# A gated mixer on one core: the u and gate columns in groups of 1024, one of four turns as seven block products

## The chip, the cores and the metric

One Trainium2 chip, one of its cores. The metric is the device time of one execution in microseconds (us), lower is better. TensorE (PE) multiplies, ScalarE (ACT) and VectorE (DVE) work element by element, GpSimd (POOL) does four small reciprocal roots, SyncE (SP) issues most of the DMAs.

## The reference, cut to what matters

Two blocks run one after the other over 256 tokens of width 2048, all in float32. The change lies in the first block:

```python
h = rmsnorm(x, a_norm)                       # (256, 2048)
z = h @ w_in                                 # w_in: (2048, 12288)
u, v, gate = jnp.split(z, 3, axis=-1)        # 4096 columns each
u = gelu(u); v = rmsnorm(gelu(v), v_gain)
sv = einsum('gpq,bnqgc->bnpgc', w_s, vc) + b_s     # 8 groups of 512 columns, chunks of 128 tokens
y = u * sv
x = x + (y * silu(gate)) @ w_out             # w_out: (4096, 2048)
```

Then follow the final norm of that block and a second block (attention, an mLSTM, a gated feed-forward net), which the change touches only in the signs of some sums.

## The kernel before

**Float32 products from three passes.** Every weight and every activation is split in a high part, rounded to TensorE's reduced float32 type (ACT, a copy), and a low part, the rest (DVE, a subtraction). A product is hi x hi + hi x lo + lo x hi: three matmuls.

**Items.** The weights come as chunks of 256 rows x 512 columns, laid out as 128 x 1024 elements (512 KB). PE goes through them as one list, ITEMS, stage by stage: v, ug, out1, vv, side, gm0 ..., down. An item of a plain chunk is 12 matmuls of 512 columns: 2 row tiles x 2 token tiles x 3 passes. A ring has RING = 4 places for w_hi and w_lo: ACT makes the high part of item n + 4 (`high_of_chunk`) once PE has ended item n (`mm_done`), DVE then makes its low part (`low_of_chunk`, L1432), and PE starts item n + 4 when `lo_ready` says so. Each engine's program is one list: what an engine does besides stands at a fixed place, behind its step for an item (`split(stage, k)` is the step that prepares item k + 4).

**Seven products for eight.** In some turns of the stages v, out1, gm0, gm1, out2 and down, four chunks (a 512 x 1024 block of weights, split as B11, B12, B21, B22) are multiplied by the Strassen-Winograd scheme: seven block products of 6 matmuls each in place of four chunks of 12. For this DVE makes four sums of weight blocks in place (`block_sum`, L1437), and the result needs sums of products: 1, 5, 6 and 7 have PSUM banks of their own (XS), and `own_products` adds them up.

**The stage ug** has none of this. Eight groups i of 512 columns: 8 chunks of u columns (PSUM banks G[0]), then 8 chunks of gate columns (G[1]). The PE side is `one("ug", ...)` with `tokens` (L556). Beside it run, per group: the high and low part of v (`v_hi`, `v_lo`) and of the scaled `w_s` (`scale_ws`, `ws_hi`, `ws_lo`); `spatial(i)`, six matmuls into SV (XS banks 2 and 3, L713); t1 = SV * gain (L1627); gelu of u straight from PSUM (ACT, L1029); t1 = (t1 + b_s) * u (L1632); tanh of the gate straight from PSUM; t2 = (t2 + 1) * gate (L1636); t1 = t1 * scale * t2, two halves (L1640), which is y; then y is turned by eight transposes (`y_turned`, L604, into TR, XS banks 0 and 1) and split in `y_high` and `y_low`.

**What is queued.** SP issues the load of a chunk into the ring place that `lo_ready` frees. Nothing else orders the engines but semaphores.

Of the kernel before, what the change touches and what calls it, by code (L numbers as in the profile page):

```python
# [5 lines left out]
P = 128  # L6
S = 256
D = 2048
# [94 lines left out]

PLAIN = ("C0", "C1", "C2", "C3")
# [5 lines left out]
for _name, _counts in PHASES:  # L110
    FIRST_ITEM[_name] = len(ITEMS)
    if _name not in WIDE_STEPS:
        ITEMS += [Item(_name, None, 0, None, None, _k) for _k in range(sum(_counts))]
        continue
# [11 lines left out]
CHUNK_ITEMS = [n for n, item in enumerate(ITEMS) if not item.product]  # L126
# [12 lines left out]

RESULT_OF = {2: 0, 4: 1, 3: 2}  # L140

GAIN_AT = {FIRST_ITEM["ug"] + (-24, -8, 14, 30, 46, 62, 78, 94)[i]: i for i in range(GROUPS)}
BLOCKS_AT = {FIRST_ITEM["v"] + 8: ("v", B11), FIRST_ITEM["v"] + 9: ("v", B12),
# [41 lines left out]

def buffer_of(q, b):

    return b if b == B21 else (b + q - quads_ahead(QUADS[q][0])) % 3


def sum_slot(phase, turn):

    return SUM_TURNS["gm0" if phase == "gm1" else phase].index(turn)
# [36 lines left out]
def group_of(phase, g):  # L230


    n = FIRST_GROUP[phase] + g
    if phase in WIDE_STEPS:
# [28 lines left out]
def build(nc, x, x_tokens, stream, w_s, params, gain_rows, final_rows, gate_w, identity, consts, out):  # L263
# [25 lines left out]
    class Wide:  # L289
# [3 lines left out]
        def __init__(self, sb, name, blocks, hi, lo, rows, sums, u):  # L293
# [8 lines left out]

    norm_in = Norm("in", "a_norm")
# [6 lines left out]
    x_junk = sb("x_junk", "y", 48 * kib, [P, 2, D])  # L310
    v_wide = Wide(sb, "v", [("y", 0), ("y", 4 * kib), ("y", 8 * kib), ("y", 12 * kib)],
                  [("y", 16 * kib), ("y", 20 * kib)], [("y", 24 * kib), ("y", 28 * kib)], ("y", 92 * kib), ("mix", 4 * kib),
                  ("y", 32 * kib))
    v_junk = sb("v_junk", "y", 48 * kib, [P, 2, COLS])

    u_act = sb("u_act", "x", 0, [P, 2, COLS])
# [5 lines left out]
    v_all = sb("v_all", "y", 64 * kib, [P, 2, E])  # L322

    v_hi = sb("v_hi", "y", 28 * kib, [P, 2, COLS], F32R)
    v_lo = sb("v_lo", "y", 60 * kib, [P, 2, COLS], F32R)
# [75 lines left out]
    wide = {"v": v_wide, "out1": out1_wide, "gm0": gm_wide, "gm1": gm_wide, "out2": out2_wide, "down": down_wide}  # L401
    u_sum = sb("u_sum", "mix", 4 * kib, [P, 4, S])

# [5 lines left out]
    ws_scaled = sb("ws_scaled", "small", off + 2 * kib, [P, 2, P])  # L409
# [62 lines left out]
    with block:  # L472

        @block.sync
        def _(sp):
# [10 lines left out]
            def load_block(q, b):  # L486

                phase, g, turn = QUADS[q]
                half = 1 if b in (B12, B22) else 0
                row = 2 * turn + (1 if b in (B22, B21) else 0)  # L490
                sp.dma_start(wide[phase].blocks[buffer_of(q, b)][:], stream[chunk_in_stream(phase, g, half, row)]).then_inc(
                    block_full[b], 16)


            for n, item in enumerate(ITEMS):
                if item.product in NEXT_IN_PLACE and quad_of(item) + 1 < len(QUADS):
                    q = quad_of(item)
                    if QUADS[q + 1][0] == item.phase:
                        sp.wait_ge(lo_ready, n + 1)
                        load_block(q + 1, NEXT_IN_PLACE[item.product])  # L500
                if not item.product and CHUNK_COUNT[n] + RING < len(CHUNK_ITEMS):
# [4 lines left out]
                if n in BLOCKS_AT:  # L506
# [15 lines left out]
                    if phase == "out1" and b == B21:  # L522

                        sp.wait_ge(sem["y_turned"], GROUPS)
# [16 lines left out]
        def _(pe):  # L541
# [87 lines left out]
            def opens_own(item):  # L629
# [3 lines left out]
                if new:  # L633
                    opened.add(key)
                    if own_ahead(item.phase, item.group):
# [23 lines left out]
            def wide_product(item, a_hi, a_lo, slot):  # L659

                p, i = item.product, sum_slot(item.phase, item.turn)
                sums = wide[item.phase]
                own = {1: 0, 5: 1, 6: 2, 7: 3}
# [34 lines left out]
            def y_turned(i):  # L698
# [5 lines left out]
                blocks_turned(t1).then_inc(sem["y_turned"], 1)  # L704

            def spatial(i):
                pe.wait_ge(sem["v_lo_ready"], i + 1)
                pe.wait_ge(sem["ws_lo_ready"], i + 1)
                if i:
                    pe.wait_ge(sem["sv_read"], i)  # L710
                for t in range(2):
                    for n, (w, a) in enumerate(((ws_hi, v_hi), (ws_hi, v_lo), (ws_lo, v_hi))):
# [3 lines left out]
            for i in range(GROUPS):  # L716
                for k in range(8):
                    one("ug", 2 * i, k, tokens("ug", 2 * i, norm_in.hi, norm_in.lo))
                    if i and k == 4:
                        y_turned(i - 1)  # L720
                if i == 0:

                    pe.wait_ge(sem["own_read"], own_ahead("ug"))
                spatial(i)
                for k in range(8):
                    one("ug", 2 * i + 1, k, tokens("ug", 2 * i + 1, norm_in.hi, norm_in.lo))
# [266 lines left out]
        def _(act):  # L993
# [3 lines left out]
            def high_of_chunk(n):  # L997

                item = ITEMS[n]
                if item.product:  # L1000
                    b, uses = PRODUCT_OF[item.product], quad_of(item)
                    of = wide[item.phase].blocks[buffer_of(uses, b)]
                    if item.product in (1, 3, 2):
                        act.wait_ge(block_full[b], 16 * (uses + 1))
                    else:
                        act.wait_ge(sem["block_sums"], 4 * uses + {5: 1, 7: 2, 6: 3, 4: 4}[item.product])
# [62 lines left out]
            def sums_high(phase, n):  # L1069

                if n - 2 in SUMS_AT[phase]:
                    i = SUMS_AT[phase].index(n - 2)
                    act.wait_ge(sem["sums_ready"], sums_ahead(phase) + i + 1)
                    activation(wide[phase].sums_hi[i][:], wide[phase].sums[:], ACT.Copy).then_inc(sem["sums_hi_ready"], 1)

            def first_product(phase, n):

                for name, g in GROUPS_BY_PRODUCTS:
# [3 lines left out]
                    if n == product_item(phase, g, turn, 6):  # L1082
                        act.wait_ge(mm_done, product_item(phase, g, turn, 1) + 1)
                        if phase == "out1" and g == 0:

                            act.wait_ge(sem["v_lo_ready"], GROUPS)
# [25 lines left out]
                        activation(wide[phase].p1[:], XS[:, 0, :], ACT.Copy).then_inc(sem["p1_ready"], 1)  # L1112

            def v_taken(q):

                product, read, _ = done("v", q)
                activation(v_all[:, :, col_block(q)], product, ACT.Copy).then_inc(read, 1)

            def v_gelu(q):

                act.wait_ge(group_read[q % 2], q // 2 + 1)
                at_v = v_all[:, :, col_block(q)]
                by_token(at_v, at_v, ACT.Gelu_apprx_tanh, scale).then_inc(sem["v_ready"], 1)

            def v_squares(q):
# [4 lines left out]
                for t in range(2):  # L1130
                    ins = activation(v_junk[:, t, :], v_all[:, t, col_block(q)], ACT.Square, accum_out=v_ss[:, t, q:q + 1])
# [39 lines left out]
            for i in range(GROUPS):  # L1171
                for k in range(16):
                    split("ug", 16 * i + k)
                    if i == 0 and k < 2:
                        v_gelu(6 + k)
                        v_squares(6 + k)
                    if k == 1:

                        if i:
                            act.wait_ge(sem["sv_ready"], i)  # L1180
                        activation(v_hi[:], v_all[:, :, col_block(i)], ACT.Copy).then_inc(sem["v_hi_ready"], 1)
                    if k == 4:
                        act.wait_ge(sem["ws_scaled"], i + 1)
                        activation(ws_hi[:], ws_scaled[:], ACT.Copy).then_inc(sem["ws_hi_ready"], 1)
                    if i and k == 4:
                        y_high(i - 1)
                    if k == 7:
                        product, read, _ = done("ug", 2 * i)
                        if i:
                            act.wait_ge(sem["u_used"], i)  # L1190
                        by_token(u_act, product, ACT.Gelu_apprx_tanh, scale).then_inc(read, 1)
                product, read, _ = done("ug", 2 * i + 1)
                if i:
                    act.wait_ge(sem["y_ready"], i)
                by_token(t2, product, ACT.Tanh, scale_half).then_inc(sem["gate_t_ready"], 1)
# [936 lines left out]
```

## Time and profile before

| | |
|---|---|
| median of 3 runs | 2097.87 us (2097.86 to 2098.11) |
| span of the profiled execution, first to last instruction | 2095.9 us |
| PE busy, LDWEIGHTS busy | 2089.8 us (100%), 1750.1 us (84%) |
| DVE busy, ACT busy | 1506.6 us (72%), 1112.4 us (53%) |
| DMA | 404.40 MB, mean 193 GB/s |

The profiled execution's time is given as its span alone. The median of the timed runs is 1.97 us above it, which is taken as what lies ahead of the first and behind the last instruction. An engine's busy time counts its instructions; matmuls overlap, so that their durations (390 ns) are longer than the distance from one to the next. In a timeline each row is a start, a duration, the engine, the line, the operation, and in brackets the idle time before it with what ended it.

### The profile page before, as it was taken

How to read it: one execution, taken by the hardware profiler on the slowest of the kernel's cores; microseconds unless marked ns; L12 is line 12 of the kernel's file. 1: busy time of each engine (PE TensorE's matmuls, PEld its weight loads, DVE VectorE, ACT ScalarE, POOL GpSimd, SP SyncE). 2: the span in 40 equal slices, each digit the busy share in tenths (PEclk: the TensorE clock that was granted, in tenths of full speed). 3: DMA queues.
4: the chain of work that ended last, by engine and by line, in shares of the span. 5: the costliest groups of instructions: out<-in, count | busy, mean ns of one | idle time of the engine just before them, and what ended most of it. 6: DMA issues, size and time to landing. Idle time of an engine off the chain costs nothing.

```text
span 2095.9 us, 25218 instructions
## 1 busy us (share of the span) xinstructions
PE 2089.8 (100%) x10000; PEld 1750.1 (84%) x10000; DVE 1506.6 (72%) x1702; ACT 1112.4 (53%) x1314; POOL 17.5 (1%) x17
## 2 busy tenths in 40 slices
PE   9999999999999999999999999999999999999999
PEld 7888888888888887888888888888888888888887
DVE  7987656655787754665669678867777777779986
ACT  6765444444456544555455454555555555555553
POOL 0000000000000000100000000000000000000000
PEclk9999999999999999999999999999999999999999
DMA  8665555555764555544465656556556566556663
GB/s 337 210 200 175 198 187 187 194 187 189 272 214 157 194 194 171 177 155 153 150 210 181 221 169 208 167 185 192 187 185 195 183 192 190 181 181 232 224 203 133
DMA packets 111957, 404.40 MB, mean 193 GB/s; under 512 B 12512, under 2 KB 13280, under 8 KB 111328
## 3 DMA queue, kind: packets, MB, share of 16 engines
q1 hardware_dynamic: 109440, 394.66, 57.1%
q10 hardware_dynamic: 2400, 8.14, 1.0%
q8 instruction: 79, 1.29, 0.3%
q14 instruction: 38, 0.31, 0.0%
HBM read 400.65 MB, written 2.10 MB: 192 GB/s over the span
## 4 chain that ended last, share of the span: by engine, by line
PE 96%; DVE 3%; ACT 1%; DMA 0%; issue 0%; ACTq 0%; DVEq 0%
PE g L556 37%; PE g L653 23%; PE xs L581 8%; PE g L581 8%; PE xs L676 5%; PE xs L585 4%; PE g L585 4%; PE g L680 4%; DVE w_lo L1432 1%; PE xs L604 1%; PE xs L713 1%; ACT w_hi L1014 0%; PE xs L833 0%; DMA xf<-in_x 0%; PE xs L830 0%
## 5 line engine op out<-in xcount | busy, mean ns | idle before, releaser
L1432 DVE TENSOR_TENSOR w_lo<-raw,w_hi 128x1024 fp32r<-128x1024 f32 x659 | 803.4, 1223 | 492.6 <-ACT w_hi L1014 486.9
L1014 ACT ACTIVATE w_hi<-raw 128x1024 fp32r<-128x1024 f32 x659 | 697.4, 1059 | 756.6 <-PE g L556 411.7
L556 PE MATMUL g<-w_hi,mid_both 128*128 128x512 f32 x1024 | 326.7, 394 | 0.0
L556 PE MATMUL g<-w_hi,in_both 128*128 128x512 f32 x1024 | 318.8, 390 | 0.1
L556 PEld LDWEIGHTS g<-w_hi,in_both 128*128 128x128 f32 x1024 | 192.2, 188 | 40.3 <-DVE v_all L1564 0.5
L556 PEld LDWEIGHTS g<-w_hi,mid_both 128*128 128x128 f32 x1024 | 192.3, 188 | 39.6
L556 PE MATMUL g<-w_lo,mid_both 128*128 128x512 f32 x512 | 199.4, 389 | 0.0
L556 PE MATMUL g<-w_lo,in_both 128*128 128x512 f32 x512 | 199.2, 389 | 0.0
L581 PE MATMUL g<-mlp_both,w_hi 128*128 128x512 f32 x704 | 176.8, 393 | 0.0
L581 PE MATMUL xs<-mlp_both,w_hi 128*128 128x512 f32 x704 | 176.3, 392 | 0.0
L581 PEld LDWEIGHTS g<-mlp_both,w_hi 128*128 128x128 f32 x704 | 126.5, 189 | 22.8
L581 PEld LDWEIGHTS xs<-mlp_both,w_hi 128*128 128x128 f32 x704 | 126.6, 189 | 22.6
L653 PE MATMUL g<-w_hi,in_both 128*128 128x512 f32 x352 | 112.6, 390 | 1.3 <-DVE w_lo L1500 1.0
L556 PEld LDWEIGHTS g<-w_lo,in_both 128*128 128x128 f32 x512 | 96.1, 188 | 19.7
L556 PEld LDWEIGHTS g<-w_lo,mid_both 128*128 128x128 f32 x512 | 96.3, 188 | 19.1
L585 PEld LDWEIGHTS g<-mlp_both,w_lo 128*128 128x128 f32 x704 | 96.2, 190 | 7.0
L585 PEld LDWEIGHTS xs<-mlp_both,w_lo 128*128 128x128 f32 x704 | 96.0, 190 | 6.9
L585 PE MATMUL g<-mlp_both,w_lo 128*128 128x256 f32 x704 | 98.3, 282 | 0.0
L585 PE MATMUL xs<-mlp_both,w_lo 128*128 128x256 f32 x704 | 98.2, 282 | 0.0
L653 PE MATMUL g<-w_hi,f_hi 128*128 128x512 f32 x240 | 93.7, 390 | 0.2
L653 PE MATMUL g<-w_hi,f_lo 128*128 128x512 f32 x240 | 93.4, 389 | 0.0
L653 PE MATMUL g<-w_lo,f_hi 128*128 128x512 f32 x240 | 93.4, 389 | 0.0
(404 smaller groups left out, 3044.3 us busy)
## 6 DMA issues: line engine op xcount, KB each, us to landing
raw<-in_stream SPq DMA_DIRECT2D x659, 512.0 KB, 3.5
d_block<-in_stream SPq DMA_DIRECT2D x28, 512.0 KB, 4.6
o_block<-in_stream SPq DMA_DIRECT2D x24, 512.0 KB, 4.7
v_block<-in_stream SPq DMA_DIRECT2D x20, 512.0 KB, 4.4
gm_block<-in_stream SPq DMA_DIRECT2D x12, 512.0 KB, 5.1
x_first<-in_x_tokens ACTq DMA_DIRECT2D x2, 1024.0 KB, 6.8
gain_row<-in_gain_rows SPq DMA_DIRECT2D x8, 256.0 KB, 3.5
xt<-in_x_tokens ACTq DMA_DIRECT2D x1, 2048.0 KB, 8.0
```

The costliest lines, as they stand in the source:

```text
L556: ins = mm(G[buf][:, t, :], a[:, kt, at_t], w[:, slot, j * COLS:(j + 1) * COLS], start=(kt == 0 and n == 0), stop=(last and j == ROWS_PER_ ...
L581: mm(UP[buf][:, b, :, :], w_hi[:, slot, j * COLS + b * P:j * COLS + (b + 1) * P], a_both[:, :, kt, :], start=(kt == 0), stop=False, skip_g ...
L585: ins = mm(UP[buf][:, b, 0, :], w_lo[:, slot, j * COLS + b * P:j * COLS + (b + 1) * P], a_both[:, 0, kt, :], start=False, stop=(last and j ...
L604: ins = turn(TR[:, b, t * P:(t + 1) * P], of[:, t, b * P:(b + 1) * P], ident[:])
L653: ins = mm(GG[:, bank, :], a[:, kt, t * P:(t + 1) * P], w[:, slot, half_chunk(j)], start=n == 0 and opens(item, bank), stop=ended and n == ...
L676: ins = mm(XS[:, own[p], :], a, w[:, slot, half_chunk(j)], start=first and opens_own(item), stop=last and j == 1 and n == 2, skip_group_ch ...
L680: ins = mm(GG[:, RESULT_OF[p], :], a, w[:, slot, half_chunk(j)], start=first and opens(item, RESULT_OF[p]), stop=False, skip_group_check=True)
L713: ins = mm(SV[:, t, :], w[:, t, :], a[:, t, :], start=(n == 0), stop=(n == 2))
L1014: activation(w_hi[:, n % RING, :], of[:], ACT.Copy).then_inc(hi_ready, 1)
L1432: v.tensor_tensor(w_lo[:, n % RING, :], of, w_hi[:, n % RING, :].bitcast(F32), ALU.subtract).then_inc(lo_ready, 1)
```

## The change

- Stage ug: per group of 512 u and 512 gate columns (1024 together) the sixteen chunks are four turns of four (C0 and C1 are u columns, C2 and C3 gate columns); turn 2 is done as seven products. 19 items in a fixed order in place of 16.
- DVE makes the four block sums of each group; products 1, 5, 6 and 7 go to banks of XS that SV and TR also use; `ug_own_products` adds them up into `act` and `gate` (SBUF), `u_result` and `gate_result` add what stands in G[0] and G[1]. gelu and tanh read those SBUF tiles, not PSUM.
- The work beside moves: `spatial(i)` from the middle of the group to behind its first item, `y_turned` behind its fourth, the last two steps of y (`gate_times`, `y_product`) from the end of a group to behind the first split of the next; `ws_scaled` falls away (ACT scales while it rounds).
- In every stage the block sums are additions where they were subtractions, with the signs of the products' sums to match; some buffers lie elsewhere.

```diff
+UG_TURN = 2
+UG_FIRST = ((0, "C0"), (0, "C1"), 1, (0, "C2"), 5, (0, "C3"), (1, "C0"), (1, "C1"), 7, 6, (1, "C2"), (1, "C3"),
+            3, 2, 4, (3, "C0"), (3, "C1"), (3, "C2"), (3, "C3"))
+UG_ORDER = ((0, "C0"), (0, "C1"), (0, "C2"), (0, "C3"), 1, (1, "C0"), 5, (1, "C1"), (1, "C2"), (1, "C3"), 7, 6,
+            (3, "C0"), (3, "C1"), 3, 2, 4, (3, "C2"), (3, "C3"))
+UG_HALF_ENDS = (16, 18)
+UG_OWN_BANK = {1: 2, 5: 3, 6: 0, 7: 1}
...
+                    if item.phase == "ug" and item.group and item.product in (1, 5):
+                        pe.wait_ge(sem["sv_read"], item.group + 1)
+                    elif item.phase == "ug" and item.group:
+                        pe.wait_ge(sem["y_lo_ready"], item.group)
...
+            for n in range(items_of("ug")):                      # PE
+                i, k = divmod(n, UG_ITEMS)
...
+                step(item, norm_in.hi, norm_in.lo, at_item % RING).then_inc(mm_done, 1)
+                if k == (0 if i else 14):
+                    spatial(i)
+                if i and k == 3:
+                    y_turned(i - 1)
...
+            for n in range(items_of("ug")):                      # ACT
+                i, k = divmod(n, UG_ITEMS)
+                split("ug", n)
...
+                first_product("ug", FIRST_ITEM["ug"] + n)
+                if k == UG_HALF_ENDS[0]:
+                    u_gelu(i)
+                if k == UG_HALF_ENDS[1]:
+                    gate_t(i)
...
-                v.tensor_tensor(to[:], a[:], b[:], ALU.subtract).then_inc(sem["block_sums"], 1)
+                v.tensor_tensor(to[:], a[:], b[:], ALU.add).then_inc(sem["block_sums"], 1)
...
+            def ug_own_products(i, k):                           # at_6 is item 11 (9 in group 0)
+                if after == 0:
+                    link(v.tensor_tensor(g.u_a, g.p1, p6, ALU.subtract))
+                if after == 1:
+                    link(v.tensor_tensor(g.u_b, p7, g.u_a, ALU.add))
+                if after == 2:
+                    link(v.tensor_tensor(g.u_a, p5, g.u_a, ALU.add))
+                if after == 3:
+                    v.tensor_tensor(g.u_d, p5, g.u_b, ALU.add).then_inc(sem["own_read"], 1)
...
+            for n in range(items_of("ug")):                      # DVE
+                i, k = divmod(n, UG_ITEMS)
+                if k == UG_HALF_ENDS[0]:
+                    u_result(i)
+                if k == UG_HALF_ENDS[1]:
+                    gate_result(i)
+                split("ug", n)
...
+                if i and k == 0:
+                    gate_times(i - 1)
+                    y_product(i - 1)
+                if k == (1 if i else 15):
+                    sv_gained(i)
+                if i and k == 4:
+                    y_low(i - 1)
+                if k == (6 if i else 16) and i + 1 < GROUPS:
+                    low(v_lo[:, i + 1], v_all[:, i + 1], v_hi[:], "v_hi_ready", i + 2, "v_lo_ready")
+                if k == (7 if i else 17) and i + 1 < GROUPS:
+                    ws_low(i + 1)
+                ug_own_products(i, k)
+                if k == 17:
+                    u_times(i)
```

`block_sums`, which `split` calls, is unchanged in its places: the first sum stands behind the low part of product 1, the second behind that of the item after it, the third behind product 5, the fourth behind product 6. `link` is an instruction followed by a wait for its own end. The last comments of some lines are put in here for the reader.

## Rows read from the trace of the kernel before

**Rows 1.** The page: busy times, TensorE's granted clock, the chain that ended last.

```profile
PE 2089.8 (100%) x10000; PEld 1750.1 (84%) x10000; DVE 1506.6 (72%) x1702; ACT 1112.4 (53%) x1314; POOL 17.5 (1%) x17
...
PEclk9999999999999999999999999999999999999999
...
PE 96%; DVE 3%; ACT 1%; DMA 0%; issue 0%; ACTq 0%; DVEq 0%
```

**Rows 2.** Busy time by engine in one ug group: length, PE, PEld, DVE, ACT.

```profile
224.22:269.99 45.77, 45.77 (x208) 37.99 (x206) 27.48 (x27) 21.45 (x23) 0.00 (x0) 1.00 0.57 190
```

**Rows 3.** Timeline of PE in the same group: transposes, six matmuls of spatial.

```profile
235.10 1.03 PE L604 MATMUL xs<-ident,t 128*128 128x128 f32 x8
...
244.15 0.39 PE L713 MATMUL xs<-v_hi,ws_hi 128*128 128x512 f32 x1
...
245.51 0.39 PE L556 MATMUL g<-w_hi,in_both 128*128 128x512 f32 x1
```

**Rows 4.** Groups of DVE instructions, whole span: busy us, mean ns, idle before.

```profile
L1437 DVE TENSOR_TENSOR v_block<-v_block,v_block 128x1024 f32<-128x1024 f32 x20 | 24.5, 1224 | 1.4
...
L1632 DVE SCALAR_TENSOR_TENSOR t<-t,par,u_act 128x1024 f32<-128x1024 f32 x8 | 10.2, 1278 | 0.0
...
L1564 DVE TENSOR_TENSOR v_all<-g,v_u 128x512 f32<-128x512 f32 x12 | 7.7, 683 | 0.7 <-DVE v_u L1554 0.5
```

**Rows 5.** Timeline of DVE in ug.

```profile
245.50 1.23 DVE L1432 TENSOR_TENSOR w_lo<-raw,w_hi 128x1024 fp32r<-128x1024 f32 x1 [1.50 <-ACT w_hi L1014]
...
269.85 1.22 DVE L1636 SCALAR_TENSOR_TENSOR t<-t,g 128x1024 f32<-128x1024 f32 x1
271.11 1.42 DVE L1640 SCALAR_TENSOR_TENSOR t<-t,scale_half,t 128x512 f32<-128x512 f32 x2
272.44 1.22 DVE L1432 TENSOR_TENSOR w_lo<-raw,w_hi 128x1024 fp32r<-128x1024 f32 x1
```

**Rows 6.** Timeline of DVE in stage v, where seven products are in use.

```profile
57.64 1.22 DVE L1432 TENSOR_TENSOR w_lo<-v_block,w_hi 128x1024 fp32r<-128x1024 f32 x1
58.96 1.23 DVE L1437 TENSOR_TENSOR v_block<-v_block,v_block 128x1024 f32<-128x1024 f32 x1
60.10 1.22 DVE L1432 TENSOR_TENSOR w_lo<-v_block,w_hi 128x1024 fp32r<-128x1024 f32 x1
...
70.39 1.23 DVE L1437 TENSOR_TENSOR v_block<-v_block,v_block 128x1024 f32<-128x1024 f32 x1
...
173.24 0.68 DVE L1546 TENSOR_TENSOR v_u<-xs,v_u 128x512 f32<-128x512 f32 x1
173.96 1.23 DVE L1432 TENSOR_TENSOR w_lo<-raw,w_hi 128x1024 fp32r<-128x1024 f32 x1
175.10 1.28 DVE L1564 TENSOR_TENSOR v_all<-g,v_u 128x512 f32<-128x512 f32 x2
```

**Rows 7.** Timeline of ACT in stages v and ug.

```profile
66.73 1.32 ACT L1029 ACTIVATE v_all<-v_all,scale 128x512 f32<-128x512 f32 x2
67.95 1.04 ACT L1014 ACTIVATE w_hi<-v_block 128x1024 fp32r<-128x1024 f32 x1
...
71.65 1.06 ACT L1014 ACTIVATE w_hi<-v_block 128x1024 fp32r<-128x1024 f32 x1 [0.47 <-DVE v_block L1437]
...
244.41 1.06 ACT L1014 ACTIVATE w_hi<-raw 128x1024 fp32r<-128x1024 f32 x1 [1.66 <-PE g L556]
```

**Rows 8.** Weight loads of PE where stage ug begins.

```profile
176.44 0.19 PEld L556 LDWEIGHTS g<-w_hi,in_both 128*128 128x128 f32 x1 [0.51 <-DVE v_all L1564]
176.55 0.19 PEld L556 LDWEIGHTS g<-w_lo,in_both 128*128 128x128 f32 x1
176.78 0.19 PEld L556 LDWEIGHTS g<-w_hi,in_both 128*128 128x128 f32 x1
```

More of the change, by code:

```diff
@@ L124, with in_ring @@
 ITEM_AT = {item: n for n, item in enumerate(ITEMS)}
-CHUNK_ITEMS = [n for n, item in enumerate(ITEMS) if not item.product]
+def in_ring(item):
+    return not item.product
+CHUNK_ITEMS = [n for n, item in enumerate(ITEMS) if in_ring(item)]
 CHUNK_COUNT = {n: c for c, n in enumerate(CHUNK_ITEMS)}
@@ L233, in group_of @@
     n = FIRST_GROUP[phase] + g
-    if phase in WIDE_STEPS:
+    if phase in WIDE:
         end = half_end(phase, g // 2, g % 2) + 1
@@ L486, in load_block @@
             def load_block(q, b):
[L488 to L492, printed above, removed]
+                phase, g, _ = QUADS[q]
+                sp.dma_start(wide(phase, g).blocks[buffer_of(q, b)][:], stream[block_row(q, b)]).then_inc(block_full[b], 16)
             for n, item in enumerate(ITEMS):
-                if item.product in NEXT_IN_PLACE and quad_of(item) + 1 < len(QUADS):
+                if next_in_place(item) is not None and quad_of(item) + 1 < len(QUADS):
                     q = quad_of(item)
@@ L661, in wide_product @@
                 p, i = item.product, sum_slot(item.phase, item.turn)
-                sums = wide[item.phase]
-                own = {1: 0, 5: 1, 6: 2, 7: 3}
+                sums = wide(item.phase, item.group)
+                own = UG_OWN_BANK if item.phase == "ug" else OWN_BANK
                 last = item.turn == last_by_products(item.phase, item.group)
@@ new lines, in v_high, with ws_high @@
+            def v_high(i):
+                if i:
+                    act.wait_ge(sem["sv_ready"], i)
+                activation(v_hi[:], v_all[:, i], ACT.Copy).then_inc(sem["v_hi_ready"], 1)
+            def ws_high(i):
+                if i:
+                    act.wait_ge(sem["sv_ready"], i)
+                else:
+                    act.wait_ge(sem["v_rstd_ready"], 1)
+                    act.wait_ge(sem["ws_in"], 16)
+                for t in range(2):
+                    ins = activation(ws_hi[:, t, :], ws_t[:, i, :], ACT.Copy, scale=v_stat[:, 4 + t:5 + t])
+                ins.then_inc(sem["ws_hi_ready"], 1)
@@ new lines, in u_gelu, with gate_t @@
+            def u_gelu(i):
+                _, end, read = group_of("ug", 2 * i)
+                act.wait_ge(group_read[0], read)
+                by_token(gated[i].act, gated[i].act, ACT.Gelu_apprx_tanh, scale).then_inc(sem["u_act_ready"], 1)
+            def gate_t(i):
+                _, end, read = group_of("ug", 2 * i + 1)
+                act.wait_ge(group_read[1], read)
+                if i:
+                    act.wait_ge(sem["y_turned"], i)
+                by_token(t2, gated[i].gate, ACT.Tanh, scale_half).then_inc(sem["gate_t_ready"], 1)
@@ L1426, in low_of_chunk @@
                 item = ITEMS[n]
-                if item.product:
-                    of = wide[item.phase].blocks[buffer_of(quad_of(item), PRODUCT_OF[item.product])][:]
+                if not in_ring(item):
+                    of = wide(item.phase, item.group).blocks[buffer_of(quad_of(item), PRODUCT_OF[item.product])][:]
                 else:
@@ new lines, in u_result, with gate_result @@
+            def u_result(i):
+                buf, end, read = group_of("ug", 2 * i)
+                dve.wait_ge(mm_done, end)
+                dve.wait_ge(sem["own_read"], own_ahead("ug", i + 1))
+                v.tensor_tensor(gated[i].act[:], G[0], gated[i].act[:], ALU.add).then_inc(group_read[0], 1)
+            def gate_result(i):
+                buf, end, read = group_of("ug", 2 * i + 1)
+                dve.wait_ge(mm_done, end)
+                v.tensor_tensor(gated[i].gate[:], G[1], gated[i].gate[:], ALU.subtract).then_inc(group_read[1], 1)
@@ L1693, in _ @@
                 if n == 0:
+                    gate_times(GROUPS - 1)
+                    y_product(GROUPS - 1)
                     dve.wait_ge(mm_done, FIRST_ITEM["out1"])
```

298 lines of the change are left out of this document (164 added, 134 removed).

## The prediction

> **What bounds the kernel now.** I read the page's busy table first: PE is busy for 100% of the span at the full granted clock, and the chain that ended last runs through PE for 96% of it [rows 1]. So time comes off only where PE issues fewer matmuls, and goes on only where PE has to wait. Then the stage windows: one ug group lasts 45.77 us, PE is busy in all of it, DVE in 27.48 us, which is 60% [rows 2]. Then the timelines, for the distances from start to start, because busy times overlap. Six matmuls of 512 columns take 245.51 - 244.15 = 1.36 us, 0.2267 each [rows 3]. Sixteen chunks of 12, 43.52 us, and `spatial`, 1.36, leave 0.89 us of the 45.77 for the eight transposes. These three are the whole group.
>
> **What the change takes off.** Four of a group's sixteen chunks (48 matmuls) become seven products of 6 (42). Six matmuls less is 1.36 us, for eight groups 48 matmuls, **10.88 us**. Nothing else of PE's work changes: `spatial` and `y_turned` move and cost the same.
>
> **What it adds on DVE.** Per group, three low parts more (19 for 16), four block sums, four sums of products of 512 columns (0.68 each), `u_result` and `gate_result` (like L1564, two halves of 0.68, here one instruction of 1024; the 1024-element rows take 1.22), less `ws_scaled` and its low part in two forms that about cancel. That is 3 x 1.22 + 4 x 1.22 + 4 x 0.68 + 2 x 1.22 = 13.7 us [rows 4, 5]. DVE goes from 27.5 to 41.2 us in a group of 44.42 (45.77 less 1.36, rounded), 93%. On average that fits. Whether PE waits hangs on the order, as neither DVE nor ACT can be more than four items ahead of PE.
>
> **Distances used.** Low part behind low part or behind a block sum 1.14 (58.96 to 60.10); block sum behind a low part, whose end it waits for, 1.32 (57.64 to 58.96); a 512-column sum with a wait for its end 0.72 (173.24 to 173.96), without one 0.60 (the pair of 1.28 less one of 0.68) [rows 4, 6]. `gate_times` to `y_product` 1.26, `y_product` to the next 1.33 (269.85, 271.11, 272.44) [rows 5]. `u_times` lasts 1.28 [rows 4], 0.09 longer than its distance of 1.19, as with the others (1.23 against 1.14). ACT begins a high part 0.26 after PE passes to the next item (244.15 to 244.41), DVE its low part 1.10 later (244.41 to 245.50), so "item n ends" to "low part of n + 4 begins" is at least 1.36 [rows 3, 5, 7]. A gelu pair from SBUF gives ACT free after 1.22 (66.73 to 67.95); ACT starts 0.03 after a DVE instruction ended (70.39 + 1.23 to 71.65) [rows 6, 7]. PE restarts 0.2 after the DVE instruction it waited for: 175.10 + 1.28 = 176.38, and the regular beat of 0.2267, reckoned back from the third weight load at 176.78, would have begun at 176.55 or a little later [rows 6, 8].
>
> **The walk through a group.** Clock 0 is PE's start of a group i of at least 1, with no wait yet. In the new order PE ends items 13 to 18 at 34.90, 36.26, 37.62, 38.98, 41.70 and 44.42. The next group's first product is due after four chunks, `spatial` and the transposes, at 44.42 + 13.13 = **57.55**. It writes SV's first bank, so it waits for `sv_gained` of its own group. Who is on the way there:
> - Low part of item 17 begins at 34.90 + 1.36 = 36.26. Third sum of products 37.40, low part 18 at 38.12, fourth sum 39.26, low part 19 at 39.86, `u_result` 41.00, ended 42.22.
> - ACT stands before its gelu of u until then: 42.25. Only behind it comes the high part of item 21, 43.47, though PE had allowed it at 41.96. DVE idles; low part 21 at 44.57, `u_times` 45.71, `gate_result` 46.90 to 48.12 (PE's last gate chunk ended at 44.42).
> - ACT stands before tanh until 48.15; the high part of item 23, which is product 1, at 49.37; its low part at 50.47.
> - Then DVE's queue: block sum 51.79, `gate_times` 52.93, `y_product` 54.19, low part 55.52, block sum 56.66, `sv_gained` 57.80 to 59.02. PE goes on at 59.22.
>
> So PE waits 59.22 - 57.55 = **1.67 us** in each group from 2 to 7, more than the 1.36 that the group saves. The walk restarts the same way in each group, as item 13's end moves with PE: the wait does not grow. Group 1 follows group 0, whose order is another (sums of products done by item 12, `sv_gained` behind item 15): `gate_result` begins 1.77 after the group's end where it is 2.48 above, so its wait is about 0.96. Every other date has room: `u_result` must be done before the next group opens its bank, 42.22 against 44.42; `y_product` before the transposes, ended 55.6 against 56.7; low parts 15, 16 and 17 before the three short products, each over 1.2 us early; low part of item 7 behind the third block sum, over 1.5 us early once PE has waited.
>
> **Group 0.** DVE comes from v with its queue full: it reads v's results at 175.10 (now) and 179.35, and the change puts two block sums there and a third behind the low part of item 4. Laid out in the same way, the low part of item 5 ends at 187.84, and PE would want it at 187.48: with the restart 0.55 us. If the sums find room, nothing.
>
> **Edits costed at nothing.** The additions for subtractions are the same instruction (1224 ns for the block sum [rows 4]); moved tiles, contiguous `v_all`, POOL's loop: same instructions, and PE's work hides them. If the tanh and gelu from SBUF cost 0.03 more each than from PSUM, the walk has it already. SP's queue: a group still loads sixteen pieces of 512 KB in about 46 us, and where it had 190 GB/s [rows 2] it has that again; block loads are issued when the old block's low part is made, over 10 us before use. For DMA, cover gone would mean waits of ACT for loads; none is due here. At the end, `gate_times` and `y_product` of group 7 go into out1, where they end near 9.9 us after its start; the transposes want them at 13.6.
>
> **Sum.** -10.88 + 6 x 1.67 + 0.96 + 0.55 = +0.65 us. Against the profiled span, 2095.9 becomes 2096.55; with the 1.97 us to the timed median, 2097.87 becomes **2098.5 us**.
>
> **Bounds.** The sum hangs on seven copies of one chain of some twenty distances. Nothing in before shows `sv_gained` as a thing PE waits for. Below: if waits at satisfied semaphores and PSUM reads come out at the cheapest rows (block sum behind low part at 1.14, restart 0.06 as the weight load shows), the chain is 0.3 shorter, twice in it 0.2, say 0.5: -3.5 us. Above: each of the five places where an engine stands for another costs 0.1 more, and the DVE idle of 0.51 before L1564 [rows 4] shows that a wait with a lone semaphore instruction can cost half a us: +0.5 to +1.0 a group, +3.5 to +7. I take the middle distances, since they are those of the same pairs of instructions.
>
> The PSUM-reading sums of 512 columns come every 0.60 to 0.72 us like SBUF ones [rows 6]. The Trainium skill ("VectorE: DVE Perf Modes", section "The TRN2 errata") gives a PSUM source 62 cycles of fixed cost more than an SBUF source, which an estimate turns into 0.065 us for each of the five such reads in the walk, 0.3 us a group and 2 us in all. By it the sum would be +2.9 us, 2100.8; the row of L1564 sides with the smaller figure.
>
> **Rivals.**
> - *The wait is not there, or small.* DVE has 7% of a group free; if the chain is shorter by over 1.4 us a group, for instance because ACT's gelu does not hold up the high part 21 (1.5 us at that place), PE never waits: 2087 to 2088 us. At a wait of 0.9 or less it is faster by over 0.2%. For it: in stage v, at a like DVE load, PE hardly waits. Against: v has no `sv_gained` and no gelu behind a DVE result on the way. Chance 0.21 for faster.
> - *The chain is longer.* Slower side: DVE is the bound from item 17 to the next group's product 1, and each 0.1 us in it costs 0.7 us. From a wait of 2.2 us a group (0.5 more) it is slower by over 0.2%, 2102.1; with 1.0 more, 2105.5. For it: five hand-overs between ACT and DVE in one chain, group by group. Chance 0.21.
> - *PE's waits come elsewhere*: v's last items and ug's first, where three block sums fall on DVE behind `v_result`. Once in the program, at most 2 to 3 us: 2101. Part of the chances above and of the middle one.
>
> **How the numbers follow.** 0.2% of 2098 is 4.2 us, about what a measurement of this kernel can tell from no change. The forecast, 2098.5, lies in the middle case, saving and waits about equal, chance 0.58. The range takes the bounds (-3.5, +7) and reaches to the rivals until 2 in 10 is left: 2090 to 2105.5.
>
> **What would show it.** In the changed kernel's trace: a ug group of about 46.1 us (44.4 if the wait is hidden); PE idle before L676's first product of a group, about 1.7 us, ended by DVE's t from xs and gain_row; seven such waits, some 11 us; DVE busy about 41 us a group; ACT idle until `u_result` and `gate_result`; 48 matmuls fewer. Wrong would be: another releaser, no idle before product 1, a group under 45.5 or over 46.7 us, or a lower granted clock.

## The result, and the profile after

The changed kernel takes **2101.97 us** in the median of 17 runs (2100.73 to 2104.12), the kernel before 2098.1 in as many. The ratio is 1.0019, with a 95% interval of 1.0012 to 1.0025: 3.9 us slower, at the edge of the 0.2% (4.2 us) that the prediction calls no difference; the interval reaches past that edge. One of before's seventeen runs took 2598.26 us, is taken for a disturbance, and moves neither the median nor the ratio. Forecast were 2098.5, range 2090 to 2105.5. The profiled execution took 2100.84 us, with a span of 2099.0 us; before's span was 2095.9.

The page of the changed kernel, busy times, granted clock and the chain that ended last [rows 1]:

```profile
PE 2081.1 (99%) x9952; PEld 1741.3 (83%) x9952; DVE 1602.3 (76%) x1798; ACT 1143.7 (54%) x1354; POOL 16.6 (1%) x17
...
PEclk9999999999999999999999999999999999999999
...
PE 87%; DVE 7%; issue 2%; ACT 2%; DMA 1%; ACTq 0%; DVEq 0%
```

PE has the 48 matmuls less (9952 for 10000) and 8.7 us less of busy time, yet the span is longer. The chain, which went through PE for 96% of the span, now spends 7% of it on DVE. Where it leaves PE is in the list of PE's waits in the changed kernel (engine, line, waited for; us in total, times, longest us):

```profile
PE xs L758 <- DVE t L1724: 10.5, 7, 1.8
PE xs L685 <- DVE ones L1600: 1.1, 1, 1.1
PE xs L797 <- DVE ge_gate L1748: 1.0, 1, 1.0
PE g L735 <- DVE w_lo L1613: 0.9, 1, 0.9
PE g L735 <- DVE w_lo L1545: 0.4, 1, 0.4
```

The two kernels differ in their line numbers. L758 is `step`'s matmul into an XS bank (L676 in the listing of before), L1724 is `sv_gained` (before's L1627), L1545 `low_of_chunk` (L1432), L1098 the high part (L1014), L797 `spatial` (L713). New or moved are L1748, the fourth sum of products, L1755 `u_result`, L1761 `gate_result` and L1729 `u_times`; L1113 is ACT's gelu and tanh. Seven waits of product 1 for `sv_gained`, one in each group from 1 on, hold most of the list. The rows of L685 and L1613 are the program's start, and before has both (1.1 and 1.0 us, at its own lines). Two groups of the stage by engine, each from one product 1 to the next (length, PE, PEld, DVE, ACT, POOL, clock, DMA, GB/s), and PE's timeline at the start of the first:

```profile
235.70:281.93 46.23, 44.68 (x200) 36.90 (x201) 39.51 (x39) 25.71 (x29) 0.00 (x0) 1.00 0.58 188
281.93:328.13 46.20, 44.64 (x200) 36.90 (x201) 39.51 (x39) 25.44 (x28) 0.00 (x0) 1.00 0.58 189
```

```profile
235.70 0.47 PE L758 MATMUL xs<-w_hi,in_both 128*128 128x512 f32 x1 [0.92 <-DVE t L1724]
236.00 0.40 PE L758 MATMUL xs<-w_lo,in_both 128*128 128x512 f32 x1
...
237.16 0.39 PE L735 MATMUL g<-w_hi,in_both 128*128 128x512 f32 x1
```

A group lasts 46.23 us, where before it was 45.77 [rows 2] and without a wait would be 44.42. The six periods from product 1 of group 1 (235.70) to that of group 7 (513.32) come to 277.62 us, 11.10 more than 6 x 44.42. DVE between them, from the low part of item 17 to the product that PE waits for (the timeline of the changed kernel):

```profile
259.00 1.23 DVE L1545 TENSOR_TENSOR w_lo<-raw,w_hi 128x1024 fp32r<-128x1024 f32 x1 [0.90 <-ACT w_hi L1098]
...
262.61 1.22 DVE L1545 TENSOR_TENSOR w_lo<-raw,w_hi 128x1024 fp32r<-128x1024 f32 x1
263.74 1.21 DVE L1755 TENSOR_TENSOR ge_act<-g,ge_act 128x1024 f32<-128x1024 f32 x1
264.87 1.21 DVE L1545 TENSOR_TENSOR w_lo<-raw,w_hi 128x1024 fp32r<-128x1024 f32 x1
267.31 1.23 DVE L1545 TENSOR_TENSOR w_lo<-raw,w_hi 128x1024 fp32r<-128x1024 f32 x1 [1.22 <-ACT w_hi L1098]
268.45 1.28 DVE L1729 SCALAR_TENSOR_TENSOR t<-t,par,ge_act 128x1024 f32<-128x1024 f32 x1
269.65 1.22 DVE L1761 TENSOR_TENSOR ge_gate<-g,ge_gate 128x1024 f32<-128x1024 f32 x1
270.78 1.21 DVE L1545 TENSOR_TENSOR w_lo<-raw,w_hi 128x1024 fp32r<-128x1024 f32 x1
273.21 1.23 DVE L1545 TENSOR_TENSOR w_lo<-ge_block,w_hi 128x1024 fp32r<-128x1024 f32 x1 [1.22 <-ACT w_hi L1098]
...
280.57 1.22 DVE L1724 TENSOR_TENSOR t<-xs,gain_row 128x1024 f32<-128x1024 f32 x1
281.70 1.22 DVE L1545 TENSOR_TENSOR w_lo<-ge_block,w_hi 128x1024 fp32r<-128x1024 f32 x1
```

DVE, the engine that PE waits for, stands idle twice for 1.22 us in this chain. Both times it waits for a high part that ACT could not begin, because ACT stood in front of its gelu or its tanh:

```profile
264.99 1.34 ACT L1113 ACTIVATE ge_act<-ge_act,scale 128x512 f32<-128x512 f32 x2 [2.01 <-DVE ge_act L1755]
266.23 2.19 ACT L1098 ACTIVATE w_hi<-raw 128x1024 fp32r<-128x1024 f32 x2
270.89 1.34 ACT L1113 ACTIVATE t<-ge_gate,scale_half 128x512 f32<-128x512 f32 x2 [2.48 <-DVE ge_gate L1761]
272.14 1.04 ACT L1098 ACTIVATE w_hi<-ge_block 128x1024 fp32r<-128x1024 f32 x1
```

Two waits outside the chain were not in the prediction. In group 0, `spatial(0)` on PE waits until the fourth sum of products (L1748) has read the bank that it writes:

```profile
207.76 0.39 PE L762 MATMUL g<-w_hi,in_both 128*128 128x512 f32 x1
209.16 0.47 PE L797 MATMUL xs<-v_hi,ws_hi 128*128 128x512 f32 x1 [1.01 <-DVE ge_gate L1748]
```

And in out1, the stage behind ug, ACT waits 6.4 us for a load of weights:

```profile
560.61 1.06 ACT L1098 ACTIVATE w_hi<-raw 128x1024 fp32r<-128x1024 f32 x1 [6.41 <-DMA raw<-in_stream]
```

PE's stretch from the start of ug to the first matmul of out1 goes from 365.5 us (176.4 to 541.9) to 368.2 (176.5 to 544.7): +2.7, and with 0.1 from before ug the traces are 2.8 us apart there. In out1 0.7 is added, where PE waits at 570.66 (0.4 us in the list of waits) some 10 us behind the ACT row above. From there to 1880 the two traces run 3.5 us apart, and 0.4 comes back behind it, which leaves the span's +3.1.

### The profile page after: what moved, and what is told of

Read it like the earlier page. It is cut to its first block, busy times and chain, and to the rows that moved or that the text cites. A ratio compares the mean times of both kernels' runs of the same rounds, so it can differ in the third digit from the quotient of the medians.

```text
span 2099.0 us, 25377 instructions
## 1 busy us (share of the span) xinstructions
PE 2081.1 (99%) x9952; PEld 1741.3 (83%) x9952; DVE 1602.3 (76%) x1798; ACT 1143.7 (54%) x1354; POOL 16.6 (1%) x17
## 4 chain that ended last, share of the span: by engine, by line
PE 87%; DVE 7%; issue 2%; ACT 2%; DMA 1%; ACTq 0%; DVEq 0%
PE g L735 29%; PE g L632 21%; PE xs L657 8%; PE g L657 8%; PE xs L758 8%; PE xs L661 4%; PE g L661 4%; PE g L762 4%; DVE w_lo L1545 2%; ACT w_hi L1098 2%; PE xs L680 1%; DMA raw<-in_stream 1%; PE xs L917 0%; DVE t L1729 0%; DVE t L1724 0%
## 5 line engine op out<-in xcount | busy, mean ns | idle before, releaser
L1545 DVE TENSOR_TENSOR w_lo<-raw,w_hi 128x1024 fp32r<-128x1024 f32 x627 | 762.9, 1222 | 376.3 <-ACT w_hi L1098 370.8
L1098 ACT ACTIVATE w_hi<-raw 128x1024 fp32r<-128x1024 f32 x627 | 663.2, 1059 | 663.1 <-PE g L632 221.9
L735 PE MATMUL g<-w_hi,in_both 128*128 128x512 f32 x1120 | 356.0, 390 | 1.4 <-DVE w_lo L1613 0.9
L735 PEld LDWEIGHTS g<-w_hi,in_both 128*128 128x128 f32 x1120 | 210.2, 188 | 47.0 <-DVE w_lo L1545 1.2
L632 PEld LDWEIGHTS g<-w_hi,mid_both 128*128 128x128 f32 x1024 | 192.3, 188 | 39.5
L735 PE MATMUL g<-w_lo,in_both 128*128 128x512 f32 x560 | 217.9, 389 | 0.0
L735 PEld LDWEIGHTS g<-w_lo,in_both 128*128 128x128 f32 x560 | 105.1, 188 | 21.7
L1098 ACT ACTIVATE w_hi<-d_block 128x1024 fp32r<-128x1024 f32 x49 | 52.0, 1061 | 56.5 <-PE g L735 39.4
```

Of the source, the lines that this page charges most:

```text
L632: ins = mm(G[buf][:, t, :], a[:, kt, at_t], w[:, slot, j * COLS:(j + 1) * COLS], start=(kt == 0 and n == 0), stop=(last and j == ROWS_PER_ ...
L735: ins = mm(GG[:, bank, :], a[:, kt, t * P:(t + 1) * P], w[:, slot, half_chunk(j)], start=n == 0 and opens(item, bank), stop=ended and n == ...
L1098: activation(w_hi[:, n % RING, :], of[:], ACT.Copy).then_inc(hi_ready, 1)
L1545: v.tensor_tensor(w_lo[:, n % RING, :], of, w_hi[:, n % RING, :].bitcast(F32), ALU.subtract).then_inc(lo_ready, 1)
```

## The experiments

Ten kernels were run; before, run again beside them, had medians of 2097.9 to 2098.1 us. Ratios are to before.

### The order on ACT: one of its two waits, the other, both

The theory is the prediction's walk: ACT is in order, and gelu and tanh stand in front of the high part of the next item. The rival is DVE's load, nearly full as it is, which would leave the time where it is as long as DVE's work is the same. The edits move only the place of an ACT instruction.

```diff
-                if k == UG_HALF_ENDS[0]:
+                if k == UG_HALF_ENDS[0] + 1:       # e1_gelu, e1_both
                     u_gelu(i)
-                if k == UG_HALF_ENDS[1]:
-                    gate_t(i)
+                if i and k == 0:                   # e1_tanh, e1_both
+                    gate_t(i - 1)
...
                 if n == 0:                         # out1
+                    gate_t(GROUPS - 1)
```

> Base is the changed kernel, 2101.97 us. Edit: ACT's gelu of u stands behind the next high part, not ahead of it. Chain theory (PE's wait at product 1 is the end of one chain through ACT and DVE): high part 21 no longer waits for u_result, the chain is 1.3 us shorter, the wait falls from about 1.85 to 0.5 us in six groups and from 1.1 to 0 in group 1: about -8.8, 2093.2. Load theory (DVE is 93% busy in ug and simply full; the order of ACT's work does not matter): within 1 us of 2102. DMA theory (late loads make the loss): within 1 us of 2102.

> Base is the changed kernel, 2101.97 us. Edit: ACT's tanh of the gate stands behind the high part of product 1, not ahead of it. Chain theory: product 1's high part no longer waits for gate_result and tanh; its low part then begins when DVE comes free, 1.3 us earlier; the same as for the gelu edit, wait 0.5 us a group, 2093.2. Load and DMA theories: 2101 to 2103.

> Base is the changed kernel, 2101.97 us. Both edits on ACT's order. Chain theory: the chain is shorter than PE's own work from item 13 to product 1, no wait is left in groups 1 to 7: -12.2, 2089.8, clearly faster than the kernel before (2098.1). Load and DMA theories: 2101 to 2103.

**Measured.** e1_gelu 2092.87 us (2092.28 to 2093.68), ratio 0.9975 [0.9965, 0.9985]; e1_tanh 2092.68 (2092.22 to 2093.55), the same ratio and interval; e1_both 2088.54 (2087.95 to 2088.86), 0.9954 [0.9941, 0.9966]. Against the changed kernel that is -9.1, -9.3 and -13.4. PE's waits for `t`, in e1_gelu, then in e1_tanh:

```profile
PE xs L758 <- DVE t L1724: 2.6, 7, 0.7
```

```profile
PE xs L758 <- DVE t L1725: 1.8, 6, 0.5
```

In e1_both the list has no such row. One of its groups, and its PE from one product 1 to the next, 44.42 us:

```profile
235.29:279.72 44.43, 44.43 (x202) 36.89 (x201) 39.55 (x39) 25.48 (x29) 0.00 (x0) 1.00 0.60 196
```

```profile
235.36 0.48 PE L758 MATMUL xs<-w_hi,in_both 128*128 128x512 f32 x1
...
279.78 0.47 PE L758 MATMUL xs<-w_hi,in_both 128*128 128x512 f32 x1
```

And ACT in the same group, where gelu now stands behind a high part that starts when PE frees its place:

```profile
264.28 1.06 ACT L1098 ACTIVATE w_hi<-raw 128x1024 fp32r<-128x1024 f32 x1 [1.66 <-PE g L735]
265.25 1.32 ACT L1113 ACTIVATE ge_act<-ge_act,scale 128x512 f32<-128x512 f32 x2
```

**What follows.** The same 39 DVE instructions, busy for 39.55 us, fit in a group of 44.43 without a wait. So the load is not the cause; the order in which ACT takes gelu, tanh and high parts is. The two parts do not add up (9.1 + 9.3 = 18.4 for 13.4), as a chain that is shortened by more than PE's wait gives nothing more. Group 1 is another case than the six groups behind it. In e1_gelu its wait is the longest that is left, 0.75 us for 0.92, where the expectation had none, and in e1_tanh it is gone: there the hand-over of the tanh makes nearly all of it.

### DVE's work on the chain and off it

One more instruction of 1024 elements per group on DVE, once between the late product-1 low part and `sv_gained`, once where PE does not wait for it; then half of it on the chain; then less work on the chain. For the last, e2_less_on leaves 960 of 1024 columns of the second block sum unsummed: it gives up part of the product, and only its time is of use.

```diff
+            def again(i):
+                dve.wait_ge(sem["sv_read"], i + 1)
+                link(v.tensor_tensor(t1[:], t1[:], t1[:], ALU.max))   # half_on: t1[:, 0]
...
+                if i and k == 6:                       # more_off
+                    again(i)
+                if i and k == 0:                       # more_on, half_on
+                    dve.wait_ge(sem["u_used"], i)
+                    again(i - 1)
                 if i and k == 0:
                     gate_times(i - 1)
...
-                    block_sum(before, B12, B22, B12)             # less_on: the second sum, in ug
+                    block_sum(before, B12, B22, B12, True)       # 64 columns of 1024
```

> Base is the changed kernel, 2101.97 us. Edit: one more DVE instruction of 1024 elements a group with a wait for its end (1.26 us), t1 = max(t1, t1), placed ahead of gate_times, on the chain to product 1. Chain theory: seven groups longer by 1.26 each: +8.8, 2110.8. Load theory: the same, +8.8.

> Base is the changed kernel, 2101.97 us. The same extra DVE instruction, placed behind the low part of item 10, where DVE later stands idle anyway, off the chain. Chain theory: nothing, 2102 within 0.7. Load theory (DVE full over the group): +8.8, 2110.8.

> Base is the changed kernel, 2101.97 us. The extra DVE instruction on the chain at half its size (512 elements, 0.72 us with its wait). In the run with the whole instruction the time rose by 15.3 us where the chain alone gives 8.8, and the trace shows TensorE at its lower clock behind PE's waits. Chain theory alone: +5.0, 2107.0. Chain and clock: PE's wait at product 1 is now about 2.6 us, between 1.85 (granted clock 1.00 in the profile) and 3.1 (0.996); a granted clock below 1.000 in most runs, stretches of the slower beat behind some of the waits, and a time above 2107.0 by what those stretches cost, 2107 to 2112, with more scatter than the 3.4 us of the changed kernel.

> Base is the changed kernel, 2101.97 us. The second of the four block sums in ug works on 64 of its 1024 columns (the rest of that block is left unsummed, part of the product is wrong): 1.0 us less on DVE, on the chain between y_product and sv_gained. Chain theory: the wait falls by 1.0 in seven groups: -7.0, 2095. Load theory (DVE full over the group): the same -7. If the wait belonged to ACT's order alone: nothing.

**Measured.** More off the chain: 2101.82 us (2101.35 to 2103.66), which is the changed kernel's time; PE's list has the same first row, in total, number and longest. Less on it: 2094.68 (2093.73 to 2095.54), -7.3. More on it: 2117.24 (2115.24 to 2118.36), ratio 1.009 [1.0077, 1.0104], that is +15.3 where +8.8 was expected; half: 2112.49 (2110.8 to 2113.65), ratio 1.0068 [1.0055, 1.008], +10.5, just above the 2107 to 2112 that was expected, with 2.9 us of scatter where more than 3.4 was expected, and a mean clock of 0.997 or 0.998 in all five runs. Of more_on's 16.7 us of additional span, the list of PE's waits holds 6.1 at product 1 (16.6 against 10.5), and 1.5 before the transposes:

```profile
PE xs L758 <- DVE t L1728: 16.6, 7, 2.4
PE xs L680 <- DVE t L1774: 1.5, 6, 0.5
```

The other 9 us are not waits. Windows of 10 us in more_on (the clock is the third figure from the end), and PE's timeline behind one of the waits:

```profile
270.00:280.00 10.00, 10.00 (x46) 8.29 (x45) 8.22 (x7) 4.80 (x7) 0.00 (x0) 1.00 0.56 174
280.00:290.00 10.00, 7.40 (x29) 5.65 (x28) 9.58 (x10) 3.84 (x4) 0.00 (x0) 0.77 0.17 55
290.00:300.00 10.00, 10.00 (x41) 8.14 (x40) 7.02 (x6) 4.96 (x7) 0.00 (x0) 0.88 0.60 180
...
380.00:390.00 10.00, 7.12 (x35) 5.55 (x34) 9.93 (x10) 3.55 (x4) 0.00 (x0) 1.00 0.16 52
```

```profile
282.81 1.09 PE L680 MATMUL xs<-ident,t 128*128 128x128 f32 x8 [0.20 <-DVE t L1774]
286.31 0.76 PE L758 MATMUL xs<-w_hi,in_both 128*128 128x512 f32 x1 [2.40 <-DVE t L1728]
...
288.57 0.63 PE L758 MATMUL xs<-w_hi,in_both 128*128 128x512 f32 x1
289.00 0.63 PE L735 MATMUL g<-w_hi,in_both 128*128 128x512 f32 x1
289.43 0.63 PE L735 MATMUL g<-w_lo,in_both 128*128 128x512 f32 x1
...
292.86 0.39 PE L735 MATMUL g<-w_lo,in_both 128*128 128x512 f32 x1
293.09 0.39 PE L735 MATMUL g<-w_hi,in_both 128*128 128x512 f32 x1
...
433.44 0.47 PE L758 MATMUL xs<-w_hi,in_both 128*128 128x512 f32 x1 [2.40 <-DVE t L1728]
...
480.91 0.47 PE L758 MATMUL xs<-w_hi,in_both 128*128 128x512 f32 x1 [2.40 <-DVE t L1728]
```

**What follows.** The same instruction costs nothing off the chain and 15.3 us on it, and work taken off the chain is given back: the position counts, not the load. Behind the wait of 2.4 us matmuls begin 0.43 apart, the 1.2 GHz level, and from 292.4 on 0.23 apart; 13 matmuls take the 5.68 us from 286.31 to 291.99, for 2.95 at the full clock, 2.7 lost. That happened behind four of the seven waits (windows below 1.00 lie around 240, 290, 340 and 530 us; the window 380 to 390 has no less idle time of PE, and 1.00).

The periods from one product 1 to the next keep the chain and the clock apart. Where the clock stays at 1.00 they are 47.47 to 47.50 us in more_on (433.44 to 480.91, for instance) and 46.95 to 46.98 in half_on, for 46.20 to 46.24 in the changed kernel without its one longer wait: +1.26 and +0.75, the length of the added instruction, as the chain theory has it. Where they begin with a drop they are 49.09, 50.30 and 49.33 in more_on and 48.80, 48.85 and 48.54 in half_on, 1.6 to 2.8 us more. Each of the two has four drops, the last of them in group 7. Four drops are about 8 us in more_on, if the last cost what the others did, and with 7 x 1.26 = 8.8 of chain they make up its 16.7. That is why half an instruction costs two thirds of a whole one: the chain's part is nearly halved, the drops are as many.

### The two places that the prediction did not see

`spatial(0)` one item later (and `sv_gained(0)` with it); the two late loads of out1 away from its start, the token load in two halves.

```diff
-                if k == (0 if i else 14):          # e3_spatial0, PE
+                if k == (0 if i else 15):
                     spatial(i)
...
-                if k == (1 if i else 15):          # e3_spatial0, DVE
+                if k == (1 if i else 16):
                     sv_gained(i)
...
-                    act.dma_start(xt[:], x_tokens).then_inc(sem["x_again"], 16)     # e4_loads
+                if n in (5, 9):
+                    t = n // 9
+                    act.dma_start(xt[:, t, :], x_tokens[:, t, :]).then_inc(sem[f"x_again{t}"], 16)
+                if n == 13:
                     act.dma_start(final_row[:], final_rows).then_inc(sem["final_in"], 16)
```

> Base is the changed kernel, 2101.97 us. Edit in group 0 alone: the six matmuls of spatial stand one item later, and t1 = SV * gain with them. The trace shows PE idle for some 1.2 us before them, until DVE's fourth sum of products has read SV's bank. If that is a loss of its own: -1.2, 2100.8, and the idle time is gone. If what follows in group 0 and 1 hangs on DVE anyway, the same time reappears before product 1 of group 1 and the run stays at 2102.

> Base is the changed kernel, 2101.97 us. Edit: the 3 MB of x and final gains that ACT loads at out1's first item go out later, in three parts behind items 5, 9 and 13. In the profile of the changed kernel ACT waits 6.4 us for a chunk of weights there and PE stands 0.8 us. If that collision is a loss of its own: about -0.8, 2101.2, no wait of PE in out1, and less scatter between runs than the 3.4 us seen. If the late loads only move, nothing.

**Measured.** e3_spatial0 2101.2 us (2099.16 to 2102.3), -0.8; e4_loads 2101.06 (2100.35 to 2102.76), -0.9. In the trace of e3_spatial0 the wait before `spatial(0)` is gone, and 0.3 us of it comes back at product 1 of group 1, which waited 0.92 us in the changed kernel:

```profile
234.71 0.47 PE L758 MATMUL xs<-w_hi,in_both 128*128 128x512 f32 x1 [1.19 <-DVE t L1724]
```

In e4_loads PE has the same seven waits at product 1 (10.5 us); ACT in out1 no longer waits for a load, and starts as soon as PE frees the place:

```profile
557.23 1.06 ACT L1098 ACTIVATE w_hi<-raw 128x1024 fp32r<-128x1024 f32 x1 [1.66 <-PE g L735]
```

**What follows.** Both places are real in the traces, but neither median moved by more than the runs scatter, so their prices rest on the traces: 1.0 us for `spatial(0)` as long as the chain stands behind it, 0.7 for out1. Nor can a single span settle them. PE begins ug at 176.4 to 177.8 us in the traces, in kernels that are alike up to there, and e4_loads has the latest start.

The loads make ACT's wait: the two kernels that move them, e4_loads and e5_all, are the only ones in which it is gone. PE's wait behind it is less firm. With the loads in their old place PE waits between 0 (e1_gelu, e1_both, e3_spatial0) and 1.7 us (e2_less_on). In before, e1_gelu and e1_both the loads are issued 3.0 to 3.1 us behind PE's start of out1, and ACT then waits at most 1.9 to 4.0 us; in the other kernels that have them in the old place it is 3.8 to 3.9 us, and ACT waits 5.6 to 6.7. That goes with the later issue, but no run moved the issue alone. e4_loads was also expected to scatter less, and did not: three of its eleven runs lie at 2102.3 to 2102.8, all with a mean granted clock of 0.999, the others at 1.000 and 2100.4 to 2101.8. So the loads are not what spreads the runs.

### All together

One kernel with all the edits that took a wait out of the trace, each as shown above: both ACT orders, `spatial(0)` later, the loads moved. No line is edited besides.

> Base is the changed kernel, 2101.97 us. The two edits on ACT's order, spatial of group 0 one item later, and the later loads together. Chain theory with both side losses: 2089.8 - 1.2 - 0.8 = 2087.8, 10 us below the kernel before; PE waits nowhere in ug but by about 0.3 us at its start. Load theory: 2100 to 2102.

**Measured.** 2087.2 us (2087.17 to 2087.46), ratio 0.9949 [0.9936, 0.9961], against 2087.8 expected. PE's list has neither a row of L758 nor of L797 left; its longest is the one at the program's start, which the changed kernel has too:

```profile
PE xs L685 <- DVE ones L1604: 1.1, 1, 1.1
```

That is 2098.1 - 10.9, the price of the 48 matmuls; by the spans of the two traces it is 10.5 (2085.4 for 2095.9). The best of the versions, it beats before by 10.9 us and the change as made by 14.8.

## Why the prediction was right, and where it was off

**What the change takes off: right.** 48 matmuls less, and e5_all shows their 10.88 us in the time, within 0.4 us, once nothing eats them.

**The walk: right in place, releaser and, nearly, in size.** Set at the low part of item 17 (36.26 of the walk is 259.00 of the trace), it puts low part 21 at 267.31 (measured 267.31), `gate_result` at 269.64 (269.65), the low part of product 1 at 273.21 (273.21), `sv_gained` at 280.54 (280.57) and PE at 281.96 (281.93). The seven waits are there, they do not grow, and the e1 runs show that each of the two ACT hand-overs which it names is in the chain of groups 2 to 7: take out either and most of the wait goes. Its size: mean 1.85 us from group 2 on, for 1.67, and 1.05 for 0.96 in group 1, together 12.2 for 11.0. In an ordinary group it is 1.81, and the missing 0.14 is made of small pieces. The restart is 0.24 to the beat where the walk has 0.20: PE starts 0.14 after the DVE instruction, and its first six matmuls take 1.46 us for 1.36. The way from PE's end of item 13 (257.58) to the low part of item 17 (259.00) is 1.42 for the 1.36 that the prediction calls the least. The rest are hundredths. One wait was 0.3 longer than the others (period 46.52): there ACT began the high part of item 17 after 1.94 us of idle time (350.55) where the other groups have 1.66, and why is open.

**Group 0: the wrong place.** The low part of item 5 cost 0.1 us, not 0.55. The wait that was missed is that of `spatial(0)`, 1.2 us: it needs the banks of products 1 and 5, and the fourth sum, which frees them, begins at 208.33 where PE had been due at 207.99. The prediction called the move of `spatial` free, and laid out group 0 on DVE only as far as the low part of item 5.

**Edits costed at nothing: one was not.** "For DMA none is due here" was wrong. ACT issues 3 MB of late loads (the tokens again, and `final_row`) near out1's start, 3.9 us behind its first matmul (548.61 - 544.72) where it was 3.0 before, and there they meet the weight stream: ACT waits 6.4 us for a chunk of weights instead of 1.9, and PE waits. In the profile that is 0.7 us. e4_loads and e5_all show that these loads make ACT's wait; why the collision is worse than before, whether by the later issue, with which it goes in the traces, or by what SP has queued then, was not tried.

**The sum.** In the stage: 12.2 + 1.2 + 0.1 - 10.88 = +2.6, for +2.7 in the traces; with 0.1 ahead of it, out1's +0.7 and -0.4 at the end +3.1, for +0.65. The median lies 1.1 us above the profiled execution besides. The term that was mis-sized is the sum of the waits in ug: 13.5 us for the 11.5 forecast (6 x 1.67 + 0.96 + 0.55), of which 1.2 is the chain and the rest `spatial(0)`, which had no term. A saving and a cost of 11 us each stand against each other, so that a tenth more of the one is a quarter of the 4.2 us at which the same ends and slower begins.

**DVE's load: right to call it no bound, too high in size.** 41.2 us a group was reckoned from durations; busy are 39.5, since instructions overlap by a tenth of their length (1.22 long, 1.13 apart). With PE's wait in it the group is 46.2 us long, so DVE is busy for 85% of it.

**The rivals.** "The wait is not there, or small" did not come. Its condition points the right way but is not enough: e1_gelu took out the hand-over that it names, and the time went 9.1 us down to 2092.9, not to 2087 or 2088, as waits of 0.26 to 0.75 us stayed. "The chain is longer, 0.7 us for each 0.1": by e2_less_on and e2_more_off the price holds (-7.3 for 1.0 us less on the chain, 0 off it). Upwards the periods at the full clock hold to it too, but the time does not, since the clock joins in. "PE's waits come elsewhere" came in part: once in the program, and of its size (1.2 + 0.1 + 0.7 us), but at `spatial(0)` and in out1, not where v ends and ug begins.

**The PSUM rule.** In the changed trace `u_result` reads PSUM and the low part ahead of it does not, yet both come 1.13 us before their successors (262.61, 263.74, 264.87), and `sv_gained` too (280.57 to 281.70). The Trainium skill ("VectorE: DVE Perf Modes", section "The TRN2 errata") gives a PSUM source 62 cycles more. The trace does not show them from start to start, and the 2100.8 us that the rule gave is nearer to the median than 2098.5 by luck: what the sum lacked were the waits that the walk had left out, and its dates are met to 0.03 us without those cycles.

**Left open.** The changed kernel's own seventeen runs scatter by 3.4 us, e5_all's five by 0.3. Of its 17 runs five have a mean clock of 0.999, and they lie at 2102.1 to 2104.1; the other twelve, at 1.000, at 2100.7 to 2102.4. In e1_gelu, e1_tanh, e1_both, e2_less_on and e5_all, where the waits are short or gone, every run has 1.000; in e2_more_off, e3_spatial0 and e4_loads, which keep them, two, three and three of eleven have 0.999. That fits clock drops behind waits of 1.8 us in some executions. It is argued from the runs' clocks only, as the one trace of the changed kernel shows 1.00 throughout.

## What to carry to other kernels

Where PE waits for an engine that is 85% busy, look first for that engine's own idle times inside the chain (here 2 x 1.22 us) and for who ends them: two instructions of a third engine, each moved behind the next piece of ring work, were worth 13.4 us, where 1.0 us less work for the busy engine in each group was worth 7.3. An in-order engine that feeds a ring should take the ring's work first, and behind it what waits for another's result. And a PE wait is dearer than its length if the clock can fall behind it, and here the version without the waits also had the least scatter.

## What the runs showed of the hardware that was not expected

- **TensorE's clock falls behind short waits.** In e2_more_on, behind a wait of 2.4 us, which followed 0.2 us of waiting and eight transposes, 13 matmuls ran 0.43 us apart, the 1.2 GHz level, instead of 0.2267. It happened behind four of seven waits of 2.2 to 2.4 us, and no row tells the four from the three. The Trainium skill ("TensorE: Matmul & The Clock Gate", section "Wait — 56ns, not 53.3ns?") has 426.7 ns for a matmul of 512 columns at 1.2 GHz, and the trace agrees; its 215.7 ns at 2.4 GHz is less than the 226.7 of these float32 passes.
- **Half an instruction on the chain cost two thirds of a whole one.** 512 elements more on DVE, +10.5 us, 1024, +15.3. A group at the full clock grew by 0.75 and 1.26 us; both traces had four drops of the clock (mean 0.997 and 0.996), and both a longest wait of 2.4 us.
- **Two late loads are enough to hold up the stream of weights.** With 3 MB issued at 548.6 us ACT waited 6.4 us for one 512 KB chunk, while over the whole program the DMA moves 193 GB/s as before. The same 3 MB in pieces, later, made it wait for none while they ran.
